# Half projections between the steps of a blocked inverse, input rows in halves, and outer products in two groups

## The reference, cut to what matters

```python
h = rmsnorm(x, g_mix)
u = h @ w_in                                    # qkv 1536, z 512, glu 1024, a, b
conv_out = silu(layernorm(depthwise31(glu(u))))  # conformer half
q, k, v, g, beta = gdn_inputs(u)                # short convolution, silu, l2 norm
# per chunk of the prompt: t_inv = inverse(I + tril(k_beta k^T * decay)), then
# u = t_inv v_beta; w = t_inv (k_beta e^g); v_new = u - w s; o = q s + intra v_new; s = ...
# sample rows: s = s*e^g + k (x) beta (v - s k);  o = s q
x = x + concat(conv_out, rmsnorm(o) * silu(z)) @ w_out
x = x + cross_attn(rmsnorm(x), mem_k, mem_v)    # prompt memory: mk, mv = rmsnorm(mem) @ w_mk, w_mv
x = x + moe(rmsnorm(x))                         # 32 experts, top 4, clamped SwiGLU
y = rmsnorm(x)
```

## Time and profile before

| | us |
|---|---|
| median of 3 runs | 1263.66 (1262.77 to 1265.44) |
| the profiled execution's own time | 1266.2 |
| its span in the profile | 1264.4 |
| TensorE busy | 1237.3 |
| VectorE, ACT, GpSimd busy | 432.7, 216.6, 31.7 |
| first projection qkv 0 starts | 13.9 |
| first step of the inverse | 82.6 |
| w_out starts | 203.7 |
| expert loop starts | 344.9 |

### The profile page before, as it was taken

The page is one execution under the profiler, slowest core; times in us unless marked ns, Lnnn a source line. Parts: engine busy times, 40 slices in busy tenths (PEclk is TensorE's granted clock), DMA queues, the critical chain, the costliest instruction groups (busy, mean ns, idle before and its releaser), DMA issues.

```text
span 1264.4 us, 18195 instructions
## 1 busy us (share of the span) xinstructions
PE 1237.3 (98%) x7187; PEld 586.8 (46%) x7187; DVE 432.7 (34%) x1267; ACT 216.6 (17%) x456; POOL 31.7 (3%) x81
## 2 busy tenths in 40 slices
PE   9999999999999999999999999999999999999997
PEld 6878747876733334333333433333333333333342
DVE  5759791373322223222222322222222233222222
ACT  3341424221311111111111111111111111111112
POOL 4000010100000000000000000000000000000000
PEclk9999899999999999999999999999999999999999
DMA  9432548599999999999999999999999999999994
GB/s 316 166 101 69 209 142 344 201 411 390 393 372 428 424 430 422 430 426 428 429 430 431 432 430 431 431 432 431 432 431 433 432 432 431 433 423 428 426 427 175
DMA packets 48901, 470.52 MB, mean 372 GB/s; under 512 B 6348, under 2 KB 6733, under 8 KB 26813
## 3 DMA queue, kind: packets, MB, share of 16 engines
q1 hardware_dynamic: 44638, 458.71, 87.1%
q0 software_dynamic: 2560, 9.80, 2.1%
q10 hardware_dynamic: 1647, 1.19, 0.3%
HBM read 463.97 MB, written 6.29 MB: 372 GB/s over the span
## 4 chain that ended last, share of the span: by engine, by line
PE 82%; DMA 15%; ACT 1%; SPq 1%; issue 0%; DVE 0%; ACTq 0%
PE banks L1246 47%; DMA ring<-in_w_gu 14%; PE banks L737 13%; PE banks L1341 5%; PE banks L1061 4%; PE banks L1324 2%; PE banks L1301 2%; PE banks L1313 1%; PE banks L1159 1%; PE banks L1186 1%; PE banks L1138 1%; DMA region_p<-in_w_dw 0%; SPq L466 0%; PE banks L1227 0%; PE banks L1456 0%
## 5 line engine op out<-in xcount | busy, mean ns | idle before, releaser
L1246 PE MATMUL banks<-ring,region_p 128*64 128x512 f32 x2208 | 488.6, 595 | 11.3 <-DMA ring<-in_w_gu 10.4
L1246 PEld LDWEIGHTS banks<-ring,region_p 128*64 128x64 f32 x2208 | 153.4, 137 | 328.5 <-issue 308.2
L2443 DVE TENSOR_SCALAR region_p<-banks 128x512 f32<-128x512 f32 x31 | 21.4, 692 | 632.4 <-PE banks L1246 632.4
L1246 PE MATMUL banks<-region_m,region_p 128*64 128x512 f32 x736 | 164.2, 595 | 3.5 <-DMA region_m<-in_w_gu 3.5
L737 PE MATMUL banks<-hT,ring 128*128 128x264 f32 (+1 forms) x512 | 117.7, 387 | 0.4 <-ACT ring L1663 0.4
L737 PEld LDWEIGHTS banks<-hT,ring 128*128 128x128 f32 x512 | 95.7, 190 | 16.3 <-ACT ring L1663 0.8
L1246 PEld LDWEIGHTS banks<-region_m,region_p 128*64 128x64 f32 x736 | 51.1, 137 | 109.1 <-issue 101.4
L2408 DVE TENSOR_TENSOR xT<-xT,banks 128x264 f32<-128x264 f32 x248 | 89.5, 423 | 0.7
L1341 PE MATMUL banks<-region_p 64*128 64x264 f32 x496 | 82.1, 415 | 0.0
L1832 ACT COPY region_p<-banks 128x264 f32<-128x264 f32 x33 | 12.5, 379 | 347.2 <-PE banks L1313 347.2
L1341 PEld LDWEIGHTS banks<-region_p 64*128 64x128 f32 x496 | 52.0, 185 | 34.8 <-issue 30.4
(11 more groups left out here) (438 smaller groups left out, 892.1 us busy)
## 6 DMA issues: line engine op xcount, KB each, us to landing
ring<-in_w_gu SPq DMA_DIRECT2D x24, 4096.0 KB, 27.2
ring<-in_w_gu SPq DMA_DIRECT2D x43, 2048.0 KB, 17.1
ring<-in_w_dn SPq DMA_DIRECT2D x12, 4096.0 KB, 29.8
ring<-in_w_dn SPq DMA_DIRECT2D x22, 2048.0 KB, 18.4
region_m<-in_w_gu SPq DMA_DIRECT2D x8, 4096.0 KB, 27.2
region_m<-in_w_gu SPq DMA_DIRECT2D x14, 2048.0 KB, 19.4
region_m<-in_w_dn SPq DMA_DIRECT2D x8, 2048.0 KB, 21.4
region_m<-in_w_dn SPq DMA_DIRECT2D x4, 4096.0 KB, 29.8
```

The costliest lines, as they stand in the source:

```text
L1246: ins = pe.matmul(bank[n][u * SLOTS:(u + 1) * SLOTS, :], lhs, rhs, start=start, stop=stop)
L2443: dve.tensor_scalar(xg, bank[0][:, :], 7.0, None, ALU.min).then_inc(sem("glu_clipped"), 1)
```

## The change

The list of jobs is rearranged, and projections can now be cut: `PARTS` says at which of the eight steps, and a `("more", key)` entry in TensorE's list resumes the job in the same bank.

- Start: the sample's rows are loaded first, and each group of 128 prompt rows in two halves of 512 columns; x_t 0 to 3 wait for the first half alone. VectorE copies x_t 0 to 3, ACT 4 to 7. Filler matmuls: seven of 256 columns ahead of x_t 0, none later before qkv 0's four. The ten parameter DMAs come directly behind the first weight group. qkv 1 goes before param.
- z 1 goes before l2 0 to 3, tail_g 2 behind kk.
- z 3, glu_b 3 and glu_a 3 are done in halves between the steps of levels 4, 5 and 6. s_krow, s_decay and s_kq go into level 6; tail_c and s_rd go behind it, between mem_t's. `conv_some` is dealt out anew.
- mk 0 is cut in three around v_new 1, state 1 and o_t 1. The outer products go four before mk 1 and four behind it.
- mv 0 goes before ln_mean. mv 1 is cut in two around ln_var. ACT does z's silu after o_norm and loads silu's table ahead of time; w_out waits for `mix` chunk by chunk.
- At the start of the loop, the first turn of gathered rows goes before the counts, and ACT copies both gathered halves before the turned ones.

```diff
+PARTS = {("z", 3): (0, 4, 8), ("glu_b", 3): (0, 4, 8), ("glu_a", 3): (0, 4, 8), ("mk", 0): (0, 2, 4, 8), ("mv", 1): (0, 4, 8)}
...
-    jobs = [("x_t", c) for c in range(6)] + [("gmix",), ("x_t", 6), ("x_t", 7), ("x_root",)]
-    jobs += [("qkv", 0), ("param", 0), ("param", 1), ("short_hist",), ("ab",), ("qkv", 1), ("ab_t",)]
-    jobs += [("qkv", 2), ("qkv", 3)] + [("conv_hist", j) for j in range(2)]
+    jobs = [("x_t", c) for c in range(4)] + [("gmix",)] + [("x_t", c) for c in range(4, 8)] + [("x_root",)]
+    jobs += [("qkv", 0), ("qkv", 1), ("param", 0), ("param", 1), ("short_hist",), ("ab",), ("qkv", 2)]
+    jobs += [("qkv", 3), ("ab_t",)] + [("conv_hist", j) for j in range(2)]
...
-    jobs += [("z", 0)] + [("l2", f) for f in (4, 5, 6, 7)] + [("tail_g", 2)]
-    jobs += [("decay_row", 0), ("decay_row", 1), ("beta_row", 0), ("beta_row", 1)]
-    jobs += [("l2", f) for f in (0, 1, 2, 3)] + [("z", 1), ("kk", 0), ("kk", 1), ("z", 2)]
+    jobs += [("z", 0)] + [("l2", f) for f in (4, 5, 6, 7)]
+    jobs += [("decay_row", 0), ("decay_row", 1), ("beta_row", 0), ("beta_row", 1), ("z", 1)]
+    jobs += [("l2", f) for f in (0, 1, 2, 3)] + [("kk", 0), ("kk", 1), ("tail_g", 2), ("z", 2)]
...
-    turned = [[], [("v_tok", 0), ("v_tok", 1)], [("qk", 0), ("qk", 1)], [("k_tok", 0)], [("k_tok", 1)], [], []]
-    solved = [[]] + [[("glu_b", i)] for i in range(4)] + [[("z", 3)], [("s_read", 0), ("s_read", 1)]]
-    merged = [[]] + [[("glu_a", i)] for i in range(4)] + [[("tail_c",), ("s_krow",), ("s_decay",), ("s_kq",)]]
+    turned = [[], [("v_tok", 0), ("v_tok", 1)], [("qk", 0), ("qk", 1)], [("k_tok", 0)], [("k_tok", 1)],
+              [("glu_b", 3)], [("more", ("glu_a", 3))]]
+    solved = [[]] + [[("glu_b", i)] for i in range(3)] + [[("z", 3)], [("more", ("glu_b", 3))]]
+    solved += [[("s_read", 0), ("s_read", 1), ("s_krow",), ("s_decay",), ("s_kq",)]]
+    merged = [[]] + [[("glu_a", i)] for i in range(3)] + [[("more", ("z", 3))], [("glu_a", 3)]]
...
-    jobs += [("s_rd",), ("w_neg",), ("v_new", 0), ("mem_t", 0), ("mem_t", 1), ("state", 0), ("o_t", 0), ("s_vrow",)]
-    jobs += [("mem_t", 2), ("mem_t", 3), ("v_new", 1), ("mem_t", 4), ("mem_t", 5), ("state", 1), ("o_t", 1)]
-    jobs += [("mem_t", 6), ("mem_t", 7), ("mk", 0)]
-    jobs += [("s_outer", g) for g in range(sample_groups)]
-    jobs += [("mk", 1), ("mk", 2)] + [("o_norm", h) for h in range(4)] + [("mk", 3), ("ln_mean",), ("mv", 0)]
-    jobs += [("mk_t", j) for j in range(4)] + [("ln_var",), ("mv", 1)]
+    jobs += [("mem_t", 0), ("mem_t", 1), ("tail_c",), ("w_neg",), ("v_new", 0), ("mem_t", 2), ("mem_t", 3), ("s_rd",)]
+    jobs += [("state", 0), ("o_t", 0), ("mem_t", 4), ("mem_t", 5), ("mk", 0), ("v_new", 1), ("more", ("mk", 0))]
+    jobs += [("s_vrow",), ("state", 1), ("o_t", 1), ("mem_t", 6), ("mem_t", 7), ("more", ("mk", 0))]
+    half = sample_groups // 2
+    jobs += [("s_outer", g) for g in range(half)] + [("mk", 1)]
+    jobs += [("s_outer", g) for g in range(half, sample_groups)]
+    jobs += [("mk", 2)] + [("o_norm", h) for h in range(4)] + [("mk", 3), ("mv", 0), ("ln_mean",)]
+    jobs += [("mk_t", j) for j in range(4)] + [("mv", 1), ("ln_var",), ("more", ("mv", 1))]
...
-            sp.dma_start(x_tok[:, 0, :], x_prompt[0, 0:P, :]).then_inc(sem("x0_in"), 16)
             sp.dma_start(x_tok[0:TS, 2, :], x_sample[:, 0, :]).then_inc(sem("xs_in"), 16)
+            for u in range(2):
+                sp.dma_start(x_tok[:, 0, 512 * u:512 * (u + 1)], x_prompt[0, 0:P, 512 * u:512 * (u + 1)]).then_inc(
+                    sem(f"x0_in{u}"), 16)
...
-            BUSY = {("x_t", 0): (4, 4), ("x_t", 2): (1, 1), ("x_t", 4): (1, 1), ("x_t", 6): (1, 1), ("x_root",): (3, 1),
-                    ("qkv", 0): (4, 1)}
+            BUSY = {("x_t", 0): (7, 2), ("qkv", 0): (4, 1)}
...
-                for k in range(KT):
+                for k in range(steps[part], steps[part + 1]):
...
-                filled(m, key)
+                if steps[part + 1] == KT:
+                    filled(m, key)
...
-                    if key[1] == 0:
-                        pe.wait_ge(sem("mix_conv"), CF)
-                        pe.wait_ge(sem("mix_gdn"), 1)
-                    project(key, 9 + key[1] // 4, key[1] % 4, mix, T)
+
+                    def mixed(k):
+                        if k < CF:
+                            pe.wait_ge(sem("mix_conv"), k + 1)
+                        else:
+                            pe.wait_ge(sem("mix_gdn"), 1)
+
+                    project(key, 9 + key[1] // 4, key[1] % 4, mix, T, mixed)
...
             first_gather()
+            first_turn(0)
             counts()
-            first_turn(0)
...
+            act.activation(zg, zg, ACT.Silu).then_inc(sem("z_silu"), 1)
+            ln_exp_table()
             mk_copy(3)
...
             inv_root(("ln_var",), T, 1.0 / (CF * P))
-            act.activation(zg, zg, ACT.Silu).then_inc(sem("z_silu"), 1)
+            act.preload_act_table(ACT.Silu)
...
-                        conv_some({2: 10, 3: 10, 4: 13, 5: 15}[lv])
+                        conv_some({2: 10, 3: 10, 4: 10, 5: 2}[lv])
...
-                        conv_some({2: 6, 3: 7, 4: 7, 5: 2}[lv])
+                        conv_some({2: 6, 3: 7, 4: 4, 5: 8}[lv])
...
+                    if i == CF - 1:
+                        conv_some(7)
```

More of the change, by code:

```diff
@@ L114, in bass_hymba_step, with between @@
         bank = [banks[:, 512 * i:512 * (i + 1)] for i in range(8)]
-        JOB = {key: n for n, key in enumerate(pre_moe_jobs(LEVELS, NG))}
+        PE_ORDER = pre_moe_jobs(LEVELS, NG)
+        JOB = {key: n for n, key in enumerate(k for k in PE_ORDER if k[0] != "more")}
         N_PRE = len(JOB)
+        ENDS = {(key[1] if key[0] == "more" else key): n for n, key in enumerate(PE_ORDER)}
+        order = sorted(ENDS, key=ENDS.get)
+        def between(first, last):
+            return order[order.index(first):order.index(last)]
         def job(key):
@@ L499, in _ @@
                         load_kv(i)
[L500 to L505, removed]
-                    sp.dma_start(rows[0:DW_ROWS, 1, :], w_dw[0].rearrange("j (f p) -> (j f) p", p=P)).then_inc(
-                        sem("param_in"), 16)
                 if g == 7:
@@ L723, in _, with project @@
         def _(pe):
-            def project(key, g, f, src, width, ready=None):
-                open_bank(pe, key)
+            def project(key, g, f, src, width, ready=None, part=0):
+                steps = PARTS.get(key, (0, KT))
+                if part == 0:
+                    open_bank(pe, key)
                 if key == ("qkv", 0):
@@ L805, in _ @@
             pe.wait_ge(sem("ones_set"), 1)
-            for key in sorted(JOB, key=JOB.get):
+            parts_done = {}
+            for key in PE_ORDER:
+                if key[0] == "more":
+                    key = key[1]
+                part = parts_done.get(key, 0)
+                parts_done[key] = part + 1
                 kind = key[0]
@@ L1062, in _ @@
                                         start=(k == 0), stop=(k == KT - 1))
-                    filled(ins, key)
+                    if steps[part + 1] == KT:
+                        filled(ins, key)
                 elif kind == "mk_t":
@@ L1547, in load @@
                 act.dma_start(dst, src).then_inc(sem(s), 16)
-            load(x_tok[:, 1, :], x_prompt[0, P:2 * P, :], "x1_in")
+            for u in range(2):
+                load(x_tok[:, 1, 512 * u:512 * (u + 1)], x_prompt[0, P:2 * P, 512 * u:512 * (u + 1)], f"x1_in{u}")
             load(rows[PR["mix"]:PR["mix"] + 8, 0, :], g_mix[0].rearrange("(c p) -> c p", p=P), "gmix_in")
@@ L1586, in _, with x_copy @@
             ln_exp_table()
-            act.wait_ge(sem("x0_in"), 16)
+            def x_copy(c):
+                wait_filled(act, "x_t", c)
+                drained(act.copy(xT[:, c, :], ps(("x_t", c))[:, 0:T]), ("x_t", c))
+            for u in range(2):
+                act.wait_ge(sem(f"x0_in{u}"), 16)
             act.activation(x_sq[:, 0, :], x_tok[:, 0, :], ACT.Square, accum_out=x_ss[:, 0:1]).then_inc(
@@ L1593, in _ @@
             act.activation(x_rs, x_rs, ACT.Exp, scale=-0.5).then_inc(sem("x_rs"), 1)
-            for c in range(2, 8):
-                wait_filled(act, "x_t", c)
-                drained(act.copy(xT[:, c, :], ps(("x_t", c))[:, 0:T]), ("x_t", c))
+            for c in range(4, 8):
+                x_copy(c)
             load(conv_rows[0:120, :, :], st_conf[0].rearrange("b j c -> (b j) c").rearrange("(a p) c -> p a c", a=2),
@@ L1657, in _ @@
             act.activation(ge, gs, ACT.Exp).then_inc(sem("ge"), 1)
-            tail_g(2)
             for c in range(NT):
@@ L1667, in _ @@
                         ("beta_row", c))
+            z_copy(1)
             inverse_lengths(0)
-            z_copy(1)
+            tail_g(2)
             z_copy(2)
@@ L1678, in glu_gate @@
                                        bias=pcol("b_glu", CF + i)), ("glu_b", i))
-            order = sorted(JOB, key=JOB.get)
```

(8 more changed lines are left out.)

52 lines of the change are left out of this document (34 added, 18 removed).

## The result

| | before | after |
|---|---|---|
| median, us | 1263.66 (1262.77 to 1265.44, 5 runs) | 1257.24 (1255.75 to 1260.47, 5 runs) |
| ratio | | 0.9949, 95% interval 0.9938 to 0.996 |
| the profiled execution: own time, span | 1266.2, 1264.4 | 1260.47, 1258.7 |
| its mean granted clock | 0.993 | 0.995 |

What follows compares the result with a forecast made beforehand. The expert-weight stream bounds the loop, and TensorE's walk ahead of it sets its start. Terms 2.7 + 0.8 + 1.07 + 4.1 + 0.3 + 0.45 = 9.4 us gave 1254.3 from 1263.66; whole range 1251 to 1260, own 1251 to 1256.

Steps and rivals of the forecast that it cites:

- The frame: Whole kernel: expert weights pace the loop; each microsecond TensorE saves ahead of it ends the kernel a microsecond earlier.
- the places that were forecast: Signs of being right: qkv 0 near 11.7, ln_mean near 185, w_out near 194.8, the loop near 335.5 us.
- start: First transposes to qkv: fewer fillers and no 0.52 parameter wait save 2.7 us, bounds 1.2 and 3.6.
- between qkv and inverse: TensorE's idle 0.37 and 0.43 for ACT's copies go, z 1 standing there: 0.8 us, bounds 0 and 1.2.
- levels: Inverse's levels 5 and 6: half projections cover waits of 0.19 and 0.88, saving 1.07 us, bounds 0 and 1.07.
- clock, 134 to 148 us: Half-clock stretches cost 5.2 us; the new order holds the clock, four fifths taken: 4.1 us, bounds 0 and 5.2.
- outer products: Sample's outer products: two groups remove mk 1's 0.31 wait for an eviction, 0.3 us, bounds 0 and 0.5.
- before w_out: ln_var's cover halves to 3.5 us against 3.2 needed; it fits by 0.3: cost 0, bounds 0 and 1.0.
- start of the loop: Expert loop's start: turn before the counts shortens the 0.82 wait for ACT's copy, 0.45 us, bounds 0.2 and 0.8.
- The 2.2 up to qkv 0: From the first transposes to qkv 0: filler 0.5, fillers before x_root 0.8, single ones 0.9, together 2.2 us.
- VectorE becomes the bound: Rival, chance 0.14: ln_mean needs VectorE's whole convolution; 2 us too much idle time cuts the gain to 7.4, 1256.3 us.
- The preloaded table: Silu's table load before w_out: w_out would wait some 0.8 us by the page; the sum used the row's 1.28.

Runs made afterwards that it cites:

- e9: The changed kernel, unchanged, profiled a second time and timed again: 1256.44 us, ratio 0.9946 to the kernel before.
- e1: The kernel before with only the start of the change (fillers, rows in halves, shared copies, parameters first, new first jobs): 1262.11 us, ratio 0.9991.
- e4: The changed kernel with the old order of levels 5 and 6, small jobs and v_new to mk 0, only mv 1 cut: 1258.13 us, ratio 0.9955.
- e5: The kernel before, unchanged, profiled a second time: 1265.28 us in its one execution.
- e6: The kernel before with only z 1 moved ahead of l2 0 to 3 and tail_g 2 behind kk 1: 1262.39 us, ratio 0.9988.
- e2: The changed kernel with the loads of wab and the short history issued ahead of the ten parameter loads: 1257.58 us, ratio 0.9951.
- e3: The changed kernel with all eight outer products in one group again, ahead of mk 1: 1260.44 us, ratio 0.9978.
- e7: The kernel before with only the new order from levels 5 and 6 to mk 0, projections in parts, outer products in two groups: 1269.81 us, ratio 1.0054.
- e11: The changed kernel with each outer-product group one mk later and convolution steps put into VectorE's gaps: 1254.53 us, ratio 0.9931.
- e12: The kernel before with four pairs of 512-column filler passes, ahead of tail_c, inv_x 6, s_rd and w_neg: 1264.77 us, ratio 1.0009.
- e10: The changed kernel with ln_mean ahead of mv 0 again, nothing else: 1265.23 us, ratio 1.0013.

## Why the prediction was right, and where its terms were off

The frame held: the stream sets the loop, its start follows TensorE, and the gain ahead of the loop comes out at the end. The sum was 9.4; 6.4 was measured, and 7.35 for e9. The sum was too large mainly by its largest term, the clock: what one execution lost was taken off the median of all. In e9's profile the places that were forecast are nearly met (w_out at 194.65 for 194.8, the loop at 334.52 for 335.5), but that is in part luck: it is the fastest execution of its five, held against a profile of the kernel before that was 2.5 above the median. Term by term, the table gives in us what the profiles show and what a usual execution gives; the last column is estimated from the profiles and medians named below it.

| term | forecast | first profiles compared | usual |
|---|---|---|---|
| start | 2.7 | 0.5 | 1.8 |
| between qkv and inverse | 0.8 | 1.75 | 1.75 |
| levels | 1.07 | 0.8 | 0.8 to 1.5 |
| clock, 134 to 148 us | 4.1 | 5.2 | 1 to 3 |
| outer products | 0.3 | -1.1 | -1.1 |
| before w_out | 0 | 0 | 0 |
| start of the loop | 0.45 | 0.47 | 0.3 to 0.5 |

The last column adds up to 4.6 to 7.5 us, and the measured 6.4 and 7.35 lie in it.

*Start.* The 2.2 up to qkv 0 was met in the first profile; over all profiles it is 1.7. The step that failed is the one that took the 0.52 wait as the kernel's own, and 0.5 for the filler: over the profiles x_t 0 starts only 0.3 earlier (6.39 in the mean against 6.65), as the filler itself takes 4.69 to 6.20 us from one execution to another, and in e9 it waited 0.23 for the input's DMA although the filler had ended.

*Between qkv and inverse.* The term was sized by the two idle rows; the start times give 1.75.

*Levels.* First inv_t to first s_outer: 79.90 less the 5.2 of the clock is 74.7, after 73.90. Worked out in the same way, e1, e4, e5 and e6 give 75.1 to 75.4, so the term is 1.2 to 1.5 there. No wait is left.

*Clock.* The mechanism was right: in the profiles, every kernel with the old order (before, e1, e4, e5, e6) fell to half clock in this stretch, none with the new one (after, e2, e3, e7 to e11). The size was taken from one execution and moved to the median; this is the term that was mis-sized most. The five profiles with the old order lost 5.1, 6.8, 3.4, 3.4 and 1.7 us to half clock here (before, e1, e4, e5, e6), but these executions were also 2.5, 5.8, 2.0, 1.1 and 0 us above the median of their kernel. Taking that off leaves 1.0 to 2.6, 1.8 in the mean, an estimate that puts the whole excess down to this stretch. e12 gives about 2. Each run's mean granted clock points the same way: 0.9980 for e9's five runs against 0.9958 for the kernel before on that chip, 0.0022 x 1255 = 2.8 us; 0.9968 against 0.9960 for e2, 1.0 us. This mean holds the router's stretch too, whose loss varies, so it is rough in both directions: e4, with the old order, has 0.9970. Only e4's median speaks for less, some 0.4, with the intervals named there.

*Outer products.* First s_outer to mk_t 0 took 32.13 before and 33.23 in both profiles after. The 0.31 wait went, but the second product of the first group now takes the bank of mk 0, which ACT has only begun to copy. I had not followed who reads that bank: its parts moved mk 0 ahead in the list, so that the second product is now the eighth job behind it. In e4, where mk 0 is whole, it is 32.13 again.

*Before w_out.* From mk_t 0 to w_out 0 it is 9.06 in both. That there was no loss with half the cover is right.

*VectorE becomes the bound.* This rival was nearer than its 0.14 says. It did not come about, but by 0.6 us. The prediction gave mv 0's new place ahead of ln_mean no term, as nothing waited there before; without it (e10) the change ends 1.4 us above the kernel before. That this part was in the change, without a term, is luck as far as the prediction goes.

Two costs had no term: the wait for the cached values in the sample's attention, 0 before, 0.67 after, but 0.78 in e5 and 0.30 in e9, so it varies between executions of either kernel; and the router's half clock, 1.7 us before and in e5, 3.4 in the first profile after, none in e9. What makes the clock fall at the router in one execution and not in another stays open, as does what sets how long it stays down.

*The preloaded table.* In the first profile after, ACT's timeline has the silu table's load at full 1.28 us and the first silu right behind it, and w_out waited for nothing:

```profile
194.35 1.28 ACT L1800 ACT_TABLE_LOAD   x1
195.66 2.10 ACT L1803 ACTIVATE mix<-region_p,late 128x264 f32<-128x264 f32 x4
```

The Trainium skill (ScalarE: Activation LUTs, What ACT_TABLE_LOAD costs) puts a switch at 2.66 us, of which 1.38 are a drain behind the load. The trace disagrees again: 1.31 us from the load's start to the silu's. The prediction's 0.8 for w_out's wait by that figure does not follow from its own terms either; 3.2 - 1.26 + 2.66 - 3.5 is 1.1.

## What to carry to other kernels

Price a wait by the time from one job's start to the next against the same jobs elsewhere, not by the idle row. Before a sum over one profiled execution is moved to the median, look at each of its large terms in a second execution: a landing time or a half-clock stretch may be its own. When the critical engine gains, work out how much the next one has to spare at each place where they meet, and move its cover first: here one job's new place, with 0.6 us to spare, stood between a gain of 0.6% and none.

## What the runs showed of the hardware that was not expected

- An idle wait of 6.08 us on TensorE cost 9.0 (e10): the granted clock was at 0.50 before the wait had ended, and 0.62 over the following 7 us. The 2.95 of e3 likewise: first s_outer to mk_t 0 takes 37.23, 4.0 more than in two groups.
- The same code loses between nothing (e9) and 3.4 us (first profile after) to half clock at the router, from one execution to the next.
- A wait of 1.75 us showed as 0.80 of idle time in the rows; the rest stood in them as longer matmuls (e6 against the kernel before).
- Four pairs of filler passes of 512 columns, set among the small blocks of 131 to 143 us, held the granted clock at 1.00 through 150 us (e12).
- The short history's small load landed at 21.67 us in one execution and before 19.73 in another of the same program.
